# Condition rows between a slot's two parts: a reordering of TensorE's work in the mixed stage of a hybrid decoder step

## What is computed

```python
ada = jnp.dot(jax.nn.silu(c), p["w_ada"]) + p["b_ada"]          # 2048 x 12288, only 9 different rows of c
sh1, sc1, gt1, sh2, sc2, gt2 = jnp.split(ada[:, None, :], 6, axis=-1)
h = _rmsnorm(x, p["g_norm1"]) * (1.0 + sc1) + sh1
... = _split_cols(jnp.dot(h, p["w_in"]))
o_gdn = gated delta rule (chunked, with a triangular solve per head)
o_dsa = sparse attention
mix = (jax.nn.sigmoid(gate_gdn) * jnp.dot(o_gdn, p["w_gdn_out"])
       + jax.nn.sigmoid(gate_dsa) * jnp.dot(o_dsa, p["w_dsa_out"]))
x = x + gt1 * jnp.dot(mix, p["w_o"])
x = x + gt2 * ffn(h2)                                            # h2 needs sh2, sc2
```

## Time and profile before

| what | before |
|---|---|
| median of 3 runs | 1908.38 us (1906.94 to 1910.01) |
| the profiled execution | 1910.28 us |
| its span | 1908.5 us |
| TensorE busy | 1853.5 us, 97% |
| GpSimd busy | 1181.0 us, 62% |
| ScalarE busy | 809.6 us, 42% |
| VectorE busy | 635.2 us, 33% |
| mean granted clock of TensorE | 0.990 |
| read from HBM | 379.70 MB, 204 GB/s over the span |

### The profile page before, as it was taken

The page is one execution under the profiler, slowest core; times in us unless marked ns, Lnnn a source line. Parts: engine busy times, 40 slices in busy tenths (PEclk is TensorE's granted clock), DMA queues, the critical chain, the costliest instruction groups (busy, mean ns, idle before and its releaser), DMA issues.

```text
span 1908.5 us, 41545 instructions
## 1 busy us (share of the span) xinstructions
PE 1853.5 (97%) x16664; PEld 1743.8 (91%) x16664; DVE 635.2 (33%) x1792; ACT 809.6 (42%) x1372; POOL 1181.0 (62%) x508
## 2 busy tenths in 40 slices
PE   6989999999999999999999999999999999999997
PEld 2679999999888878888999999999999999999996
DVE  3225654443423332323533523321133221122333
ACT  3354445655423232324434655543344443344442
POOL 0357666665434434436876677777777777777773
PEclk9999999999999999999999999999999999999998
DMA  9986654443787878789765455555555455454552
GB/s 391 407 295 200 193 159 143 145 151 131 243 293 255 302 253 298 236 277 305 237 223 168 145 166 167 165 167 166 167 166 166 166 167 165 165 166 165 165 183 83
DMA packets 145662, 391.29 MB, mean 205 GB/s; under 512 B 27778, under 2 KB 36498, under 8 KB 144882
## 3 DMA queue, kind: packets, MB, share of 16 engines
q1 hardware_dynamic: 125536, 374.62, 58.2%
q10 hardware_dynamic: 19986, 14.70, 2.5%
HBM read 379.70 MB, written 8.88 MB: 204 GB/s over the span
## 4 chain that ended last, share of the span: by engine, by line
PE 91%; DMA 4%; DVE 3%; issue 1%; POOL 1%; ACT 1%; DVEq 0%; SPq 0%; ACTq 0%; POOLq 0%; PEldq 0%
PE bank L2462 27%; PE bank L2463 26%; PE bank L2467 26%; PE bank L2422 3%; DMA raw_a<-in_stream 2%; DMA raw_c<-in_stream 1%; PE bank L2965 1%; PE bank L2411 1%; PE bank L2396 1%; DMA raw_e<-in_stream 0%; POOL rest_a L869 0%; PE bank L2850 0%; PE bank L2699 0%; PE bank L2834 0%; DVE x L2386 0%
## 5 line engine op out<-in xcount | busy, mean ns | idle before, releaser
L869 POOL TENSOR_TENSOR rest_a<-raw_a,hi_a 128x1024 fp32r<-128x1024 f32 (+1 forms) x168 | 398.7, 2375 | 238.5 <-ACT hi_a L934 237.7
L2462 PE MATMUL bank<-h_hi,hi_a 128*128 128x288 f32 x1696 | 470.0, 303 | 5.1 <-ACT hi_a L934 4.6
L2463 PE MATMUL bank<-h_lo,hi_a 128*128 128x288 f32 x1696 | 460.2, 297 | 0.0
L2462 PEld LDWEIGHTS bank<-h_hi,hi_a 128*128 128x128 f32 x1696 | 321.8, 190 | 23.5 <-issue 17.9
L2463 PEld LDWEIGHTS bank<-h_lo,hi_a 128*128 128x128 f32 x1696 | 322.8, 190 | 0.2
L934 ACT ACTIVATE hi_a<-raw_a 128x1024 fp32r<-128x1024 f32 x165 | 174.6, 1060 | 280.4 <-PE bank L2467 209.7
L869 POOL TENSOR_TENSOR rest_b<-raw_b,hi_a 128x1024 fp32r<-128x1024 f32 x74 | 178.1, 2407 | 109.1 <-ACT hi_a L934 108.9
L2467 PE MATMUL bank<-h_hi,rest_a 128*128 128x288 f32 x1456 | 221.6, 294 | 1.3 <-POOL rest_a L869 1.3
L2467 PEld LDWEIGHTS bank<-h_hi,rest_a 128*128 128x128 f32 x1456 | 202.5, 188 | 1.8 <-POOL rest_a L869 1.8
L2462 PE MATMUL bank<-h_hi,hi_b 128*128 128x288 f32 x640 | 173.9, 298 | 0.0
L2463 PE MATMUL bank<-h_lo,hi_b 128*128 128x288 f32 x640 | 172.1, 295 | 0.0
(11 more groups left out here) (546 smaller groups left out, 3793.6 us busy)
## 6 DMA issues: line engine op xcount, KB each, us to landing
raw_a<-in_stream SPq DMA_DIRECT2D x364, 512.0 KB, 3.6
raw_b<-in_stream SPq DMA_DIRECT2D x179, 512.0 KB, 3.6
raw_c<-in_stream SPq DMA_DIRECT2D x94, 512.0 KB, 3.4
raw_m<-in_stream SPq DMA_DIRECT2D x27, 512.0 KB, 5.8
raw_e<-in_stream SPq DMA_DIRECT2D x12, 512.0 KB, 9.8
st<-in_state ACTq DMA_DIRECT2D x8, 512.0 KB, 5.8
st<-in_state SPq DMA_DIRECT2D x8, 512.0 KB, 6.5
out_state_s<-st ACTq DMA_DIRECT2D x8, 512.0 KB, 6.3
```

The lines of the kernel that those rows point to most:

```text
L869: nc.gpsimd.tensor_tensor(rest_in(name, r)[:, :, cols], raw_of(name, r)[:, :, cols], w_hi[q].bitcast(f32)[:, :, cols], ALU.subtract).then_ ...
L2462: MM(banks[c][:, 0:N], w_, hi_of(k), start=(first and k == 0), stop=False)
L2463: ins = MM(banks[c][:, 0:N], w_, lo_of(k), start=False, stop=False)
```

## The change

`slot` is cut in two, `high_part` with the 16 products of rounded weights and `rest_part` with the 8 of the rests, and goes on calling both everywhere but in the mixed stage. There a gap is now filled by `fill_gap` as a whole. Where a gap has both a D slot and row slots, rows run between the two parts: in a gap that begins with D all of them; in a gap in which rows come first the last of them, the others staying ahead; and in a gap with rows first whose D is followed by a fold, none. Waits and signals stay with the instructions they stood at.

```diff
-            def slot(name, j, hi_of, lo_of, banks, first, last_, i=0, per=0, tiles=None):
-
-                r, _ = raw_at(name, j, i, per)
+            def high_part(name, j, hi_of, lo_of, banks, first, i=0, per=0, tiles=None):
+
                 q, cnt = split_at(name, j, i, per)
                 pe.wait_ge(hi_ready, cnt + 1)
...
+            def rest_part(name, j, hi_of, banks, last_, i=0, per=0):
+
+                r, _ = raw_at(name, j, i, per)
                 wait_rest(name, j, i, per)
...
+            def slot(name, j, hi_of, lo_of, banks, first, last_, i=0, per=0, tiles=None):
+
+                high_part(name, j, hi_of, lo_of, banks, first, i, per, tiles)
+                rest_part(name, j, hi_of, banks, last_, i, per)
...
+            def fill_gap(js, done):
+
+                rows = [j for j in js if KIND[j][0] == "A"]
+                slots = [KIND[j][1] for j in js if KIND[j][0] == "D"]
+                if not slots:
+                    ahead = len(rows)
+                elif KIND[js[0]][0] == "D":
+                    ahead = 0
+                elif D_AT[slots[0]] in TURN_AT:
+                    ahead = len(rows)
                 else:
...
+                    ahead = len(rows) - 1
+                for j in rows[:ahead]:
+                    cond_rows(j, *divmod(KIND[j][1], AS))
+                for i in slots[0:1]:
+                    fill_high(i)
+                for j in rows[ahead:]:
+                    cond_rows(j, *divmod(KIND[j][1], AS))
+                for i in slots[0:1]:
+                    fill_rest(i, done)
...
-                for j in GAPS[p]:
-                    fill(j, done)
-                    turned += j in TURN_AT
+                fill_gap(GAPS[p], done)
+                turned += sum(j in TURN_AT for j in GAPS[p])
```

More of the change, by code:

```diff
@@ L2462, in slot @@
                         MM(banks[c][:, 0:N], w_, hi_of(k), start=(first and k == 0), stop=False)
-                        ins = MM(banks[c][:, 0:N], w_, lo_of(k), start=False, stop=False)
+                        MM(banks[c][:, 0:N], w_, lo_of(k), start=False, stop=False)
+            def rest_part(name, j, hi_of, banks, last_, i=0, per=0):
+                r, _ = raw_at(name, j, i, per)
                 wait_rest(name, j, i, per)
@@ L2769, in _, with fill_high @@
             dh, dl = (lambda k: do_r[:, k, :]), (lambda k: do_r[:, LO_TILE[k], :])
[L2771 to L2775, removed]
-                else:
[L2777 to L2791, removed]
+            def fill_high(i):
+                n, s_ = D_SLOTS[i]
+                what, m, size = D_GROUPS[n]
+                if i == 0:
+                    bs, cnt = grp("in", 2, N_IN - 1)
+                    pe.wait_ge(grp_free[bs], cnt + 2)
+                elif s_ == 0:
+                    before, m0, _ = D_GROUPS[n - 1]
+                    if before == "ds":
+                        pe.wait_ge(pd_done, m0 + 1)
+                    else:
+                        pe.wait_ge(g_sig, m0 + 1 + (KT // CT if before == "gg" else 0))
+                a_hi, a_lo = (dh, dl) if what == "ds" else (hh, hl)
+                high_part("mix", D_AT[i], lambda k: a_hi(s_ * KS + k), lambda k: a_lo(s_ * KS + k), (bank[0], bank[1]), s_ == 0)
@@ new lines, in fill_rest @@
+            def fill_rest(i, done):
+                n, s_ = D_SLOTS[i]
+                what, m, size = D_GROUPS[n]
+                a_hi = dh if what == "ds" else hh
+                rest_part("mix", D_AT[i], lambda k: a_hi(s_ * KS + k), (bank[0], bank[1]), s_ == size - 1)
+                if D_AT[i] in TURN_AT:
+                    fill_turn(TURN_AT[D_AT[i]], done)
+            def fill_gap(js, done):
[7 more added lines that the diff above has]
+                    ahead = len(rows)
+                else:
+                    ahead = len(rows) - 1
[7 more added lines that the diff above has]
+                    fill_rest(i, done)
+                for i in slots[1:]:
+                    fill_high(i)
+                    fill_rest(i, done)
```

## The result

The changed kernel takes 1914.41 us in the median of 7 runs (1912.8 to 1916.29), the kernel before 1907.28 us in 7 runs beside it (1905.69 to 1910.01). The ratio is 1.0028, with a 95% interval of 1.0017 to 1.004: slower, by a little more than runs can tell from no change.

A forecast was written before the change was run, and what follows sets the result against it. TensorE, busy for 97% of the span, was taken as the bound. Borders +7.6, waits for rests -2.1, group ends +1.5 and loads +0.8 summed to +7.8 us, so 1916.2 us, range 1909.6 to 1923 us.

The forecast's parts named there:

- points 1 to 4: Mixed stage: ends of wide blocks +3.2, ends of row blocks +1.2, wide behind narrow +4.3, pair/quad steps -1.1; sum +7.6 us.
- The rival by which the weights of the rests would be loaded while the rows still run: Inside split slots of the mixed stage: borders cost nothing, sum +0.2 us, 1908.6 us; chance 0.09.
- point 3: Mixed stage: in 43 slots the first product with rests now follows narrow rows, 0.10 us each, +4.3 us.
- point 4: Wide pair and quad steps: 6 fewer followed by rows, 6 fewer behind rows, 12 x 0.09, -1.1 us.
- point 5: Gaps 24 and 45: rows fill 1.07 us of each wait for GpSimd's rests, -2.1 us; bounds 0 and 3.3 us.
- point 6: Three group ends with one short step behind: the next group waits 0.5 us longer each for its banks, +1.5 us.
- point 7: Loads near the mixed stage's end: buffers come free later, 0 to 1.6 us, middle taken, +0.8 us.

The follow-up runs named there:

- D D A A A A: Kernel before with fillers reordered to two D slots, then mostly four row slots: ratio 1.0004; with the square root also behind the rests: 0.9991.

## Why the prediction was right

The forecast was 7.8 us more and 1916.2 us; measured were 7.1 us between the medians, 5.3 us by the ratio, and 6.0 us between the two profiled executions (1910.28 and 1916.29).

1. Borders, forecast +7.6 us (points 1 to 4): busy time less half clock rose by 7.7 us. Each of the three prices stood in the new trace as it had been read from the old one, 0.09 at the end of a wide block, 0.10 at the end of rows, 0.10 at the first wide product behind. The rival by which the weights of the rests would be loaded while the rows still run fell: 0.10 us was paid there in all 43 places (0.235 to 0.241 us from the first product with rests to the second), and the load of the weights began only with the product. So the row decides over the rule on pulling weights ahead in the Trainium skill (TensorE: Matmul & The Clock Gate, Part 2, step 1); the one on the drain at a change of tiling mode (TensorEngine Tiling, Key Properties) agrees with the rows here, at 0.09 to 0.10 us a side. Counted again in the traces the borders come to 7.5 us: point 3 leaves out that four of the H stood behind something narrow before and no longer do (-0.4), point 4 that three more wide steps are now followed by narrow ones (+0.3); the two nearly cancel.
2. Waits for rests, forecast -2.1 us with 0.4 and 0.8 us left (point 5): 3.0 us fell to 1.1 us in two waits, the longer 0.7, so 1.9 us. (The forecast counted from start to start, 3.3 us for both, which takes in the end of the product ahead; the list counts idle time alone.) The run with the root behind the rests shows that the root was the cause.
3. Group ends, forecast +1.5 us at three places (point 6): three waits, 0.5, 0.4 and 0.4 us, 1.3 in all, at those three gaps.
4. Loads, forecast +0.8 us out of 0 to 1.6 (point 7): nothing. TensorE came later by as much as the loads did, so the last slots kept 0.23 and 0.42 us of cover. So the true size was the lower bound and not the middle, and the argument for it stood in the same paragraph.
5. Half clock: it stayed where it was, behind the wait for the fold in a gap that is not split. That it comes and goes from one execution to the next was not in the forecast, and at 1.5 us it is as large as the smaller terms; that it cost the same before and after was luck.

The sum in these sizes: 7.7 - 1.9 + 1.3 = +7.1 us, against 6.45 us of the stage; the difference is the wait ahead of a pair step (2.5 us before, 1.8 after).

## What to carry to other kernels

In this kernel a change on TensorE between products with full 128 by 128 weights and products in strips or tiles cost about 0.1 us on either side, even where nothing waited. Before moving small work into a wait, count the borders that it adds, and set them against the waits that it covers: here 43 cuts covered two waits. If only two places wait, cut two places, or take away what makes them wait; and if small pieces must run between large ones, gather them into few long runs, and look at what the longer runs do to the other waits. The runs here could not tell the gain of cutting two places, or of moving the root, from none; the profiles show that the waits went.

## What the runs showed of the hardware that I had not expected

In 7 of the 12 profiles the granted clock falls to half for 3.4 or 6.8 us within the mixed stage, although TensorE is over 97% busy in it. Ahead of each fall TensorE had been idle in one wait: of 0.9 to 1.6 us, ended 0.8 to 2.0 us before the fall, or, in the two kernels D D A A A A, of 2.2 and 2.5 us, with the fall inside it. The reverse does not hold. The kernel before has six other waits of 0.9 to 1.7 us with no fall behind them, and three profiles have the wait of 1.3 us for the fold and no fall in the stage. In the kernel with the root behind the rests (stretches ahead of and in the fall; the second number is TensorE's busy time, PEclk the third from the end):

```profile
684.10:687.50 3.40, 1.83 (x22) 0.73 (x14) 3.33 (x12) 3.34 (x4) 2.02 (x1) 1.00 0.64 160
687.50:690.90 3.40, 3.40 (x18) 3.40 (x15) 1.51 (x4) 0.15 (x1) 2.66 (x2) 0.50 1.02 399
```

So a wait of 0.9 to 1.6 us can cost 1.5 us more behind it, and a single profile of such a kernel is uncertain by that much. There is one profile of each kernel, so where the falls lie in its other executions isn't shown; the mean granted clock of whole executions of the kernel before ranged from 0.985 to 0.993.
